# Turning attention probabilities by VectorE squares and DRAM instead of by TensorE, in a two-layer hybrid attention trunk

## The reference

```python
def hybrid_layer(x, ...):
    h = rms_norm(x, pre_w)
    dq, dk, dv, dg, sq, sk, sv, sg, iq, ik, iw = split(h @ w_in)      # 8 parts of 512, iq 512, ik 64, iw 8
    # differential attention, 4 heads, two 64-wide q/k maps per head
    p = softmax(causal(rope(dq) @ rope(dk).T * scale))                # per head and map
    oa = rms_norm((p[0] - lam * p[1]) @ dv) * (1 - lambda_init) * silu(dg)
    # sparse attention: an indexer of 8 heads picks 64 keys per query
    score = sum_heads(relu(rope(iq) @ rope(layer_norm(ik)).T) * iw)   # causal
    ob = softmax(sq_roped @ sk_roped[top 64 of score].T * scale) @ sv[top 64] * silu(sg)
    y = concat(oa, ob) @ w_out
    return x + rms_norm(y, post_w)
```

## Time and profile before

| | |
|---|---|
| median of three runs | 304.04 us |
| the profiled execution | 303.62 us |
| its span, first to last instruction | 301.8 us |
| PE busy | 295.1 us, 98% |
| PEld busy | 249.6 us, 83% |
| DVE busy | 235.2 us, 78% |
| ACT busy | 164.1 us, 54% |
| POOL busy | 69.2 us, 23% |
| DMA | 56.87 MB, mean 188 GB/s |
| granted TensorE clock | 0.997 |

### The profile page before, as it was taken

The page is one execution under the profiler, slowest core; times in us unless marked ns, Lnnn a source line. Parts: engine busy times, 40 slices in busy tenths (PEclk is TensorE's granted clock), DMA queues, the critical chain, the costliest instruction groups (busy, mean ns, idle before and its releaser), DMA issues.

```text
span 301.8 us, 4431 instructions
## 1 busy us (share of the span) xinstructions
PE 295.1 (98%) x1592; PEld 249.6 (83%) x1592; DVE 235.2 (78%) x476; ACT 164.1 (54%) x284; POOL 69.2 (23%) x116
## 2 busy tenths in 40 slices
PE   8999999999999999999999999999999999999992
PEld 8799777788787888888888988778878788888892
DVE  4753989799999987973984786878999999778333
ACT  5886853645677464503665855473737747370101
POOL 6558500303031120001070740011303031110101
PEclk9999999999999999999999999999999999999998
DMA  7999959457519578221059799947653775300011
GB/s 252 367 370 386 368 210 365 139 125 241 201 43 233 185 247 311 64 59 38 0 156 369 246 348 246 294 144 197 208 151 129 140 279 156 125 2 0 0 72 70
DMA packets 49110, 56.87 MB, mean 188 GB/s; under 512 B 21952, under 2 KB 26816, under 8 KB 49088
## 3 DMA queue, kind: packets, MB, share of 16 engines
q1 hardware_dynamic: 48800, 56.33, 57.7%
q10 hardware_dynamic: 288, 0.26, 0.3%
HBM read 52.91 MB, written 3.67 MB: 187 GB/s over the span
## 4 chain that ended last, share of the span: by engine, by line
PE 98%; DVE 0%; POOLq 0%; issue 0%; DVEq 0%; ACT 0%; POOL 0%; ACTq 0%
PE bank_a L437 20%; PE bank_a L446 20%; PE bank_a L442 20%; PE bank_a L595 7%; PE bank_s L595 6%; PE bank_t L416 4%; PE bank_a L454 4%; PE bank_o L572 4%; PE bank_s L555 2%; PE bank_s L535 1%; PE bank_s L547 1%; PE bank_o L724 1%; PE bank_t L595 1%; PE bank_o L446 1%; PE bank_s L446 1%; PE bank_o L442 1%
## 5 line engine op out<-in xcount | busy, mean ns | idle before, releaser
L965 DVE TENSOR_TENSOR w_lo<-w_raw,w_hi 128x2048 fp32r<-128x2048 f32 (+1 forms) x46 | 98.4, 2149 | 18.0 <-ACT w_hi L741 17.7
L741 ACT ACTIVATE w_hi<-w_raw 128x2048 fp32r<-128x2048 f32 (+1 forms) x46 | 81.9, 1784 | 32.3 <-PE bank_a L446 24.0
L437 PE MATMUL bank_a<-w_hi,h_hi 128*128 128x512 f32 (+1 forms) x272 | 72.7, 389 | 0.0
L446 PE MATMUL bank_a<-w_lo,h_hi 128*128 128x512 f32 (+1 forms) x272 | 70.1, 379 | 0.0
L442 PE MATMUL bank_a<-w_hi,h_lo 128*128 128x512 f32 (+1 forms) x272 | 70.0, 379 | 0.0
L446 PEld LDWEIGHTS bank_a<-w_lo,h_hi 128*128 128x128 f32 x272 | 49.6, 188 | 10.3 <-DVE w_lo L965 0.8
L442 PEld LDWEIGHTS bank_a<-w_hi,h_lo 128*128 128x128 f32 x272 | 49.8, 188 | 9.8
L437 PEld LDWEIGHTS bank_a<-w_hi,h_hi 128*128 128x128 f32 x272 | 47.8, 188 | 10.3 <-issue 2.7
L809 ACT ACTIVATE xt_pbuf<-xt_pbuf,st 128x128 f32<-128x128 f32 (+1 forms) x48 | 21.2, 444 | 24.0 <-DVE st L1097 24.0
L1391 POOL TENSOR_TENSOR rt<-nat,tab 128x256 f32<-128x256 f32 x10 | 7.4, 742 | 112.2 <-ACT nat L793 112.1
L793 ACT ACTIVATE nat<-bank_a,st 128x512 f32<-128x512 f32 x20 | 13.5, 681 | 19.6 <-PE bank_a L446 19.6
(11 more groups left out here) (194 smaller groups left out, 444.9 us busy)
## 6 DMA issues: line engine op xcount, KB each, us to landing
w_raw<-in_w_in SPq DMA_DIRECT2D x30, 1024.0 KB, 6.0
w_raw<-in_w_out SPq DMA_DIRECT2D x8, 1024.0 KB, 6.1
w_raw<-in_w_in SPq DMA_DIRECT2D x8, 584.0 KB, 7.5
turned<-mixn SPq DMA_DIRECT2D x20, 128.0 KB, 2.7
prm<-in_rows SPq DMA_DIRECT2D x2, 705.0 KB, 7.0
w_raw<-in_w_in SPq DMA_DIRECT2D x2, 512.0 KB, 6.4
xres<-in_x SPq DMA_DIRECT2D x2, 512.0 KB, 9.6
dqT<-turned SPq DMA_DIRECT2D x2, 512.0 KB, 5.8
```

What stands on the lines that cost most here:

```text
L437: pe.matmul(bank, h_hi[:, HALF * half + kk, tok], whi[:, kk, :], start=half == 0 and kk == 0, stop=False)
L446: mm = pe.matmul(bank, h_hi[:, HALF * half + kk, tok], wlo[:, kk, :], start=False, stop=half == 1 and kk == HALF - 1)
L741: act.activation(unit(w_hi, u), unit(raw, u), ACT.Copy).then_inc(hi_done.sem, 1)
L965: dve.tensor_tensor(unit(w_lo, u), unit(raw, u), unit(w_hi, u).bitcast(F32), ALU.subtract).then_inc(lo_done.sem, 1)
```

## The change

Every turn of probabilities leaves TensorE. VectorE transposes their squares (`turn_probs`, now a VectorE function: 128x512 for `PD0`, `PD1A`, `PD1B`, `PS0`, and 128x1024 for `PS1`, which joins both halves), SP writes them to DRAM and reads them back (`put_probs`, `get_probs`) into `pT`. The differential keys `DK` take the same way. The six drains of probabilities and the two of `DK` go from VectorE's list. The squares of `SQ` go to the tile `iqT` instead of `mixn`.

The chunks are renumbered: `DQ` and `DK` come ahead of `DG` and `SG`, so in layer 0 the two chunks behind the opening four groups are 512 wide, and the 292-wide `DG` comes later. The turn of the indexer key comes one group earlier, the index scores before `first(8)` instead of behind it. VectorE's list is rearranged (index key statistics earlier, the last three `choose` rounds behind `mask_scores(12)`), half of the rotary tables move ahead of the first root on GpSimd, and `values(3)` moves from ahead of `out_part(1,0,0)` to behind it.

The core of the diff:

```diff
-IQ, MIXED, DG, SG, DQ, DK, SQ, SK, DV, SV = range(10)
+IQ, MIXED, DQ, DK, DG, SG, SQ, SK, DV, SV = range(10)
...
+            def put_probs(layer, n):
+                sp.wait_ge(prob_squares.sem, prob_squares.at(layer, n - PD0 + 1))
+                put(n, prob_buf[n], prob_put[n].sem)
+
+            def get_probs(layer, n):
+                sp.wait_ge(prob_put[n].sem, prob_put[n].at(layer, 16 * SQUARES))
+                slots = {PD0: pT[:, 0, :], PD1A: pT[:, 1, :], PD1B: pT[:, 2, :], PS0: pT[:, 0, :],
+                         PS1: pT[:, 1:3, :].rearrange("p s n -> p (s n)")}
+                if n >= PS0:
+                    sp.wait_ge(o_filled.sem, o_filled.at(layer, 1 if n == PS0 else 2))
+                sp.dma_start(slots[n], scratch[n].rearrange("p a t -> p (a t)")).then_inc(prob_landed[n].sem, 16)
...
+                    if u == 11:
+                        sp.wait_ge(dk_squares.sem, dk_squares.at(layer, 1))
+                        put(DKS, squares, dk_put.sem)
...
                     if u == 17:
                         sp.wait_ge(sq_put.sem, sq_put.at(layer, 16 * SQUARES))
-                        get(2, sqT, sq_landed.sem)
+                        get(SQS, sqT, sq_landed.sem)
+                        put_probs(layer, PD0)
+                    if u == 18:
+                        get_probs(layer, PD0)
+                        put_probs(layer, PD1A)
+                        put_probs(layer, PD1B)
+                    if u == 19:
+                        get_probs(layer, PD1A)
+                        get_probs(layer, PD1B)
...
+                for u in range(RING):
+                    if u == 0:
+                        put_probs(layer, PS0)
+                    if u == 1:
+                        get_probs(layer, PS0)
+                    if u == 2:
+                        put_probs(layer, PS1)
+                        get_probs(layer, PS1)
+                    if layer < DEPTH - 1:
...
# TensorE
-                turn_nat(T_DK, 0, 3)
                 first(13)
...
-                turn_probs(T_PD0, 6, 0, HEADS)
                 diff_scores(10, 1, (2, 3))
                 second(15)
-                turn_probs(T_PD1A, 8, 1, 2)
                 first(16)
                 second(16)
                 turn_nat(T_SK, 0, 5)
                 first(17)
-                turn_probs(T_PD1B, 10, 1, 2)
...
                 turn_mix(T_MD0, 0, 0)
                 first(19)
-                turn_probs(T_PS0, 12, 0, HEADS)
                 second(19)
                 turn_mix(T_MD1, 1, 1)
-                values(2, 0, v_dsa, ..., T_PS0 + 1, place(layer, SV, 0) + 1)
-                turn_probs(T_PS1A, 13, 1, 2)
+                values(2, 0, v_dsa, ..., (PS0,), place(layer, SV, 0) + 1)
                 out_part(0, 0, 0)
-                turn_probs(T_PS1B, 14, 1, 2)
                 turn_mix(T_MS0, 0, 2)
                 out_part(0, 0, 1)
-                values(3, 1, v_dsa, ...)
                 out_part(1, 0, 0)
+                values(3, 1, v_dsa, ..., (PS1,), place(layer, SV, 1) + 1)
                 out_part(1, 0, 1).then_inc(y_done.sem, 1)
...
# VectorE, from the sparse keys on
                 drain_pair(T_SK, skT)
                 split_lo(layer, 18)
-                drain(T_PD1B, pT[:, 2, :])
                 mask_scores(12, 0, 4, work[0][:, :])
+                choose(1, 3)
+                mask_unchosen(1)
                 split_lo(layer, 19)
+                turn_probs(PS0, 12)
                 split_lo(layer, 20)
                 gate_diff(0)
...
                 mask_scores(13, 1, 2, work[1][:, :])
                 mask_scores(14, 1, 2, work[1][:, :])
+                turn_probs(PS1, 14)
                 drain_mix(T_MD0, m_hi, m_lo, 0, subln)
                 gate_diff(1)
-                drain(T_PS0, pT[:, 0, :])
                 split_lo(layer, 22)
                 drain_mix(T_MD1, m_hi, m_lo, 1, subln)
-                drain(T_PS1A, pT[:, 1, :])
                 gate_dsa(0)
-                drain(T_PS1B, pT[:, 2, :])
                 drain_mix(T_MS0, h_hi, h_lo, 0)
```

More of the change, by code:

```diff
@@ L86 @@
 ROW_N = sum(ROW.values())
-T_IK, T_DK, T_PD0, T_PD1A, T_SK, T_PD1B = 4, 5, 7, 8, 9, 11
-T_MD0, T_PS0, T_MD1, T_PS1A, T_PS1B, T_MS0, T_MS1 = 12, 13, 14, 15, 16, 17, 18
-T_USES = 19
+T_IK, T_SK, T_MD0, T_MD1, T_MS0, T_MS1 = 4, 5, 7, 8, 9, 10
+T_USES = 11
+IQS, DQS, DKS, SQS = range(4)
+PD0, PD1A, PD1B, PS0, PS1 = range(4, 9)
 LANES = 32
@@ L174, in build_trunk @@
         squares = mixn[:, :, :].rearrange("p b n -> p (b n)")
+        sq_buf = iqT[:, :, :, :].rearrange("p b f t -> p (b f t)")
+        prob_buf = {PD0: mixn[:, 0, :], PD1A: nat[:, 1, 0, :], PD1B: nat[:, 1, 1, :],
+                    PS0: dkT[:, 0:2, :].rearrange("p f t -> p (f t)"), PS1: dqT[:, :, :, :].rearrange("p b f t -> p (b f t)")}
         A = [pb("bank_a0", [P, WIDTH]), pb("bank_a1", [P, WIDTH])]
@@ L681, in body @@
                 values(1, 1, v_diff, [[slot(1 + h // 2, 2 * (h % 2) + t) for t in range(2)] for h in range(HEADS)],
-                       T_PD1B + 1, place(layer, DV, 1) + 1)
+                       (PD1A, PD1B), place(layer, DV, 1) + 1)
                 second(18)
@@ L702, in body @@
                 out_part(0, 0, 1)
-                values(3, 1, v_dsa, [[slot(1 + h // 2, 2 * (h % 2) + t) for t in range(2)] for h in range(HEADS)],
-                       T_PS1B + 1, place(layer, SV, 1) + 1)
                 pe.wait_ge(t_drained.sem, t_drained.at(layer, T_MS0 + 1))
                 out_part(1, 0, 0)
+                values(3, 1, v_dsa, [[slot(1 + h // 2, 2 * (h % 2) + t) for t in range(2)] for h in range(HEADS)],
+                       (PS1,), place(layer, SV, 1) + 1)
                 out_part(1, 0, 1).then_inc(y_done.sem, 1)
@@ L1013, in turn_squares, with turn_probs @@
                     dve.wait_ge(rope_done.sem, rope_done.at(layer, rope))
-                    dve.transpose(squares, nat[:, slot, :, :].rearrange("p b n -> p (b n)")).then_inc(done, 1)
+                    dve.transpose(sq_buf if rope == 4 else squares, nat[:, slot, :, :].rearrange("p b n -> p (b n)")).then_inc(done, 1)
+                def turn_probs(n, use):
+                    if n >= PS0:
+                        dve.wait_ge(exps_done.sem, exps_done.at(layer, use + 1 - S_DIFF0))
+                    else:
+                        dve.wait_ge(combined.sem, combined.at(layer, n - PD0 + 1))
+                    probs = pbuf[:, 1:3, :].rearrange("p s n -> p (s n)") if n == PS1 else pbuf[:, use % 4, :]
+                    dve.transpose(prob_buf[n], probs).then_inc(prob_squares.sem, 1)
                 def drain_mix(j, dst_hi, dst_lo, b, weight=None):
@@ L1168, in body @@
                 split_lo(layer, 5)
-                split_lo(layer, 6)
+                key_stats()
                 dve.wait_ge(prm_landed.sem, prm_landed.at(layer, 16))
@@ L1441, in _ @@
             rotary_angles()
+            rotary_tables((0, IDX_HEADS, HD, 0))
             root_x(0, 0)
@@ L1478 @@
     result = nc.dram_tensor("out", (1, SEQ, D_MODEL), F32, kind="ExternalOutput").ap()
-    scratch = [nc.dram_tensor(f"turned{i}", (P, BLOCKS * HEADS, P), F32).ap() for i in range(3)]
+    scratch = [nc.dram_tensor(f"turned{i}", (P, HEADS if PD0 <= i <= PS0 else BLOCKS * HEADS, P), F32).ap() for i in range(PS1 + 1)]
     build_trunk(nc, *args, scratch, result)
```

173 lines of the change are left out of this document (89 added, 84 removed).

## The result

The changed kernel takes 306.56 us (median of four runs, 305.82 to 307.26); the kernel before, on the same chip, 303.97 (303.71 to 304.04). The ratio is 1.0084, 95% interval 1.0061 to 1.0108: slower by 2.6 us, where 300.5 was forecast.

The account below looks back on a forecast made before the run. TensorE, busy 98% of the span, was taken as the bound. Per-layer gains of 2.2 us ahead of the scores, less 0.3 at the end, twice, plus 0.1, less 0.4, gave 304.04 - 3.5 = 300.5 us; range 298.2 to 302.5.

Parts of the forecast that it names:

- Ahead of `dsa_scores(12)`: Before the sparse scores, TensorE loses `DK`, `T_PD0`, `T_PD1A` and `T_PD1B`: 2.2 us less per layer.
- The opening: Layer 0 start: larger units 4 and 5 land later; net 0.4 us lost, bounds nothing and 2.3.
- VectorE keeps up ahead of the sparse scores: Before `dsa_scores(12)`: VectorE's changed list is in time with 0.9 us of cover; nothing charged.
- The end of a layer: `dsa_scores(12)` to T_MS0: VectorE's list sets 25.2 us instead of 24.93, a loss of 0.3 per layer.
- two waits of 0.8: End of a layer: TensorE waits 0.8 us for `gate_diff(1)` at T_MD1 and 0.8 for `gate_dsa(0)` at T_MS0.
- the cover for late trips: End of a layer: 1.6 us of TensorE waits for VectorE, which late round trips could fill without cost.
- bring nothing: Behind `dsa_scores(12)`: removing turns `T_PS0`, `T_PS1A`, `T_PS1B`, 1.3 us per layer on TensorE, gains no time.
- The round trips: Probabilities written to DRAM and read back: `PD0` up to 1.6 us late at `values(0)`, charged 0.
- Its sum for `PD0`: From start of the `SQ` writes to `PD0`'s landing: 14.0 to 16.9 us, wanted by `values(0)` at 15.3.
- `PD1B` has about 2 us to spare: Round trip of `PD1B` through DRAM: estimated to land about 2 us before it is wanted.
- Lateness costs nothing.: Behind `dsa_scores(12)`: trips up to 1.6 us late only fill an equal wait set by VectorE.
- Rival B: Round trips through DRAM late by more than 1.6 us; 302.5 at 1 us per layer beyond the cover; chance 0.13.

Follow-up runs that it names:

- e1: Changed kernel plus 24 extra matmuls on the identity, read by nobody, between `dsa_scores(12)` and `values(0)` on TensorE; 308.45 us.
- e2: Changed kernel with `values(0)` issued behind the output part `second(17)` instead of ahead of it; 309.64 us.
- e3: Changed kernel with `PD0`'s probabilities read back from DRAM ahead of the load of unit 21 in SP's order, not behind it; 313.72 us.
- e5: e2 plus two exchanges on VectorE: `drain_mix(T_MD0)` ahead of the squares of `PS1`, `gate_dsa(0)` ahead of `drain_mix(T_MD1)`; 308.60 us.
- f3: Changed kernel with loads of units 20 to 22 cut to 256 KB from 1024 KB each, instructions unchanged, output not the reference's; 300.44 us.
- f4: Changed kernel with 10 extra matmuls between `dsa_scores(12)` and `values(0)`, where e1 has 24; 306.84 us.
- f1: Changed kernel with `PD0`, `PD1A` and `PD1B` turned on TensorE again at their old places; sparse turns and `DK` still through DRAM; 306.48 us.
- g3: f2 with `T_PS0`, `T_PS1A` and `T_PS1B` also back on TensorE in their old places; 305.50 us.
- f2: Changed kernel with only `PD0` turned on TensorE again, ahead of `diff_scores(10)`; 302.50 us.

## Why the prediction was wrong, step by step

- **Ahead of `dsa_scores(12)`, 2.2 us per layer.** Right. 1.87 less in layer 0, where the opening takes its part. From T_MS0 of layer 0 to `dsa_scores(12)` of layer 1 it took 248.26 - 130.24 = 118.02 us, before 249.04 - 128.79 = 120.25: 2.23 less.
- **The opening, 0.4 lost.** Right to within what the runs tell apart. In this trace it is 2.2 - 1.87 = 0.33; over the seven kernels with the same opening (changed, e1, e2, e3, e5, f3, f4) `dsa_scores(12)` starts at 101.99 to 102.50, so 0.3 to 0.8 is lost. TensorE is late for the low weights of units 4 and 5 by 0.3 and 0.4 us here, in f3 for high ones too (0.5), and the waits of the earlier trace rows are gone. So f3's 300.44 is closer to 300.5 than its terms are: its opening took 0.4 more than forecast, and its two stretches 0.4 less.
- **VectorE keeps up ahead of the sparse scores.** Right: no wait for it there in the changed kernel. f1 shows how narrow it is.
- **The end of a layer, 25.2 instead of 24.93.** Right as a sum: 25.02 in f3, where the DMA engines have room. Of the two waits of 0.8 in it 0.50 and 0.60 came, so the cover for late trips was 1.1, not 1.6. The wording that the three turns "bring nothing" was wrong for the changed lists: with the turns back on TensorE (g3) the stretch is 1.4 us longer per layer, at least 0.9 of it through them. The change also moved three `choose` rounds of 0.98 us into the same VectorE list; that these cost what the turns give follows from the sum and isn't shown, since no run has them alone.
- **The round trips, "I take 0".** This is the step that failed. Its sum for `PD0` gave 14.0 to 16.9 us behind the start of the `SQ` writes and 17.3 were measured: the landing of the writes took 4.6 where the sum had 2.5, and the four 64 KB writes 2.90 of issue, just over the upper end of "1.4 to 2.8". The load took 1.92 instead of 0.7, but that cost nothing: SP was through with it at 98.95 and waited for the writes until 100.60. The lead was short too, 101.99 - 88.13 = 13.9 us where 14.4 was taken. Together `PD0` was 2.5 us late, where up to 1.6 was allowed. The greater error was in the sentence that had no sum: "`PD1B` has about 2 us to spare" by "the same steps". It was 3.9 us late (12.9 against 9.0). Each landing was taken from a trace in which the DMA engines had pauses (a share of 0.14 from 102 to 106 us), and the prediction never added up what they must carry. The rows give that sum, as an estimate. The writes of `SQ`, `PD0` and `PD1` are 1280 KB, at 146 GB/s 9.0 us; the loads of units 20 to 22 are 3 MB, at 387 GB/s 8.1; the reads of `SQ`, `PD0` and `PD1` are 1280 KB, 3.4 at the same rate. That is 20.5 us of full engines, and from 90, when the first writes flow, until `PD1` was wanted at 101.99 + 9.0 = 111.0 are 21. Nothing was left for the latencies of three trips that wait for each other.
- **"Lateness costs nothing."** Wrong, since it was more than the cover. `values(1)` starts 13.30 us behind `dsa_scores(12)` instead of 8.99 (f3), 4.3 late; 1.1 of that is covered, and 3.2 are left, the 28.25 - 25.02 of the stretch. A TensorE that stands still also falls to the lower clock, which the prediction didn't have: another 1.7 us (5.38 against 3.65 in e1). In the changed kernel that cost nothing by itself, since it lies ahead of the landing of `PD1` (f4); in e2 it lies behind it and costs 1.66.
- **Rival B** named the mechanism and the sign in the profile, at 0.13, and worked it out at 1 us per layer beyond the cover. The measured 28.25 - 25.02 = 3.2 us per layer account for 306.56 - 300.44 = 6.1 us, 3.1 per layer.

A page spoke against the step. The Trainium skill, DMA: Bandwidth & Descriptors, "Specifications", asks for 512 B and more per transfer for full rate. The trace agrees with it: with the engines full, 128-byte writes flow at 146 GB/s and weights at 387. The prediction had the rule, and its 190 GB/s from the issue time was near the flow in its own trace (181 GB/s from 91.00 to 92.50, at a share of 1.06), but it used the rate for the time of one trip and never as a load on engines that others need.

One thing it could not have had from its rows: in the changed kernel the writes of `SQ` flow slower than before, at 144 GB/s in the same window with a share of 0.96, and in layer 1 at 139 (236.30 to 237.80) where it was 184 (237.00 to 238.30). In layer 0 their read is issued 5.6 us behind their start instead of 5.1; in layer 1 it is 5.5 in both kernels. The change took the squares of `SQ` from `mixn` to `iqT`. That this is the reason isn't shown, since no run puts them back.

## What to carry to other kernels

When a change puts new transfers into a stretch, add up the time that all its DMAs need at the rates of their own run lengths, not only the latency of the one that is waited for; landings read from a trace with pauses hold only while the pauses last. When one wait is found, ask what stands next in the same queue before removing it: here the first wait hid a longer one, and taking it away alone made the kernel slower. And a wait of TensorE can cost more than itself when the clock falls behind it: ahead of another wait that is nothing (f4), behind the last one it counts in full (e2).

## What the runs showed of the hardware that was not expected

- Writes of 128-byte runs hold the DMA engines at a share of 0.97 while moving 146 GB/s (181 at 1.06 in the kernel before). Four writes of 64 KB take SP as long to issue (2.90 us) as four of 128 KB (3.00). Eight of 64 KB took 5.28 us in f3, with the engines at a share of 0.61, and 8.35 in f2, at 0.92.
- A TensorE wait of 2.41 us was followed by a granted clock of 0.52 for 3.5 us, one of 4.31 (e3) by 0.50 for 3.4 us, and one of 1.38 (e3) by none:

```profile
104.80:108.56 3.76, 3.76 (x21) 3.26 (x22) 3.55 (x10) 1.28 (x8) 0.00 (x0) 1.00 1.10 306
117.48:120.88 3.40, 3.40 (x16) 3.40 (x17) 1.95 (x9) 2.07 (x8) 0.00 (x0) 0.50 1.03 251
```

  The Trainium skill, TensorE: Matmul & The Clock Gate, "HAM oscillation — how this bites in real kernels", describes waits for a DMA that bring the lower clock back. The waits of 2.41 and 4.31 us agree; behind the one of 1.38 the clock stayed.
- Work on matrices that nobody reads kept the clock from halving (granted 1.00 behind it in e1, 0.95 in f4, whose profiled execution has 0.95 from end to end), but saved no time here: f4's time is set by `PD1`, and e1's extra work was itself too long.
